# Gated delta rule on Trainium2: key lengths by one-column products, keys turned once, diagonal blocks packed by TensorE before and after one block transpose

## The chip, the cores and the metric

The kernel runs on one core of one Trainium2 chip, in one launch. The metric is the device time of the launch in microseconds. The kernel before took 861.17 us as the median of 3 runs (860.39 to 863.37).

## The reference, cut to what matters

The program is two residual blocks at model width 1024 over 256 tokens, in float32. The first block has two layers: an attention layer and a gated delta-rule layer with 8 heads of width 128. The second block is a wide mixer with a feed-forward network. The change is almost all inside the delta-rule layer.

```python
q = l2_normalize(...); k = l2_normalize(...)          # x * rsqrt(sum(x*x) + 1e-6), per token and head
...
lmat = einsum('bhncd,bhnjd->bhncj', k * beta, k) * decay_strict   # C x C per chunk, C = 64
a_mat = lmat + eye(C)
sol = triangular_solve(a_mat, [v*beta, k*beta*exp(g_cum)], lower=True, unit_diagonal=True)
u, w = sol[..., :Dv], sol[..., Dv:]
a_qk = einsum('bhncd,bhnjd->bhncj', q, k) * decay_incl
for each chunk:  v_new = u - w @ state;  o = (q*exp(g)) @ state + a_qk @ v_new
                 state = state*exp(g_last) + (k*exp(g_last - g)).T @ v_new
```

The kernel works with chunks of 128 tokens, so that there are 16 matrices of 128x128 (8 heads, 2 halves of the sequence). It inverts each triangular matrix by blocks: the 16x16 blocks on the diagonal by VectorE, for all matrices at once, and the larger blocks by products on TensorE.

## The kernel before, in words

The matrices that are multiplied by weights are split in two parts. ScalarE casts each unit of weights (128x1024) to a rounded high part (L1240), VectorE subtracts for the low part (L1838), and TensorE adds three products of 8 matmuls each (L387, and for the last eight units of the stage gdn_in L821, called z_unit 24 to 31). Four slots for the parts go round, and the order of all work is written out by hand on each engine. Each engine runs its instructions in that order, and counting semaphores tie them.

**Before the layer.** After the stage moba_out, GpSimd issues four DMAs of 1 MB each (`late_in`, L2543), with a semaphore for each. TensorE multiplies each of them (`late_products`, L765): number 0 and 1, then `add_partitions` (L617, products of a 128x128 operand with one column of ones), `sum_squares` (L472), and later number 2 and 3.

**The 24 units of q, k and v.** For each unit, ScalarE copies the product to `cin` and to `proj`, and VectorE adds three shifted copies, a short convolution (L2086), before it makes the low part of the unit four further on. After units 17 and 18 ScalarE applies silu to the keys (L1452), after 19 and 20 to the queries.

**The order on TensorE behind unit 23.** Keys turned (natural_k 0, four 128x128 transposes, L838), the decay rows spread over the partitions (L858), natural_k 1, z 24, natural_k 2 and 3, z 25, key-by-key products (gram_k, L868), z 26, values turned (natural_v, L887), z 27, the keys turned a second time (natural_k_again, L848), z 28, z 29, the first key-by-query products (L879), and then the products that turn the inverses (L928). These wait for the diagonal blocks from VectorE (`gdn_scattered`). From there on TensorE builds up the inverses (L939 to L985) between z 30 and z 31, and then the outputs.

**The order on ScalarE there.** A table load, four exponentials (L1492), the key lengths as 16 squares with an accumulator read each (L1478), logarithm and roots of the lengths (L1520 to L1522), the decay exponentials (L1498), z 24 taken out, a table load and silu of the values (L1452), z 25, four copies of 32 partitions for `ct` (L1537), z 26, the values scaled (L1504, these wait for natural_v), z 27, the decayed keys (L1511, these wait for natural_k_again), z 28 and 29.

**The order on VectorE there.** The last convolution and the low part of unit 27, the decay differences (L2126), the triangular matrices `lt` (L2143), the low parts of units 28 and 29, then four block transposes of 32 partitions by 512 elements each, which gather the diagonal blocks (L2153), the small inversions (L2165 to L2202), and four block transposes back into `tt` (L2206).

Of the kernel before, what the change touches and what calls it, by code (L numbers as in the profile page):

```python
# [36 lines left out]
P = 128  # L37
D = 1024
KT = D // P
S = 256  # L40
# [55 lines left out]
for _name, _count in PARAMS:  # L96
# [6 lines left out]
          ("pick", 31), ("parity", 4)]  # L103
# [16 lines left out]
def _program(nc, io, ctx):  # L120
# [34 lines left out]
    def after(name, n):  # L155

        return sem(name), n + start.get(name, 0)
# [53 lines left out]
    cin = [area((S + 3) * u, S + 3) for u in range(GROUP)]  # L211
# [167 lines left out]
    def _(pe):  # L379
# [449 lines left out]

        def natural_k(g):  # L830

            pe.wait_ge(*after("gdn_silu", g // 2 + 1))
            if g < 2:
                pe.wait_ge(taken, all_taken("gdn_in", 23 + g))
            else:
                pe.wait_ge(*after("gdn_length", g - 1))
            for j in range(4):
                mm = pe.transpose(ps[:, 2 + g % 2, j * P:(j + 1) * P], block(8, g, j), ident)  # L838
            mm.then_inc(sem("gdn_natk"), 1)

        def natural_k_again(g):

            if g < 2:
                pe.wait_ge(*after("gdn_length", 3 + g))
            else:
                pe.wait_ge(*after("gdn_vb", 4 * (g + 1)))
            for j in range(4):
                mm = pe.transpose(ps[:, 2 + g, j * P:(j + 1) * P], block(8, g, j), ident)  # L848
            mm.then_inc(sem("gdn_natk"), 1)
# [32 lines left out]
        def natural_v(g):  # L882

            pe.wait_ge(*after("gdn_silu", 4 + g // 2 + 1))
            pe.wait_ge(*after("gdn_lt", g + 1))
            for j in range(4):
                mm = pe.transpose(ps[:, SPREAD[g], j * P:(j + 1) * P], block(16, g, j), ident)  # L887
            mm.then_inc(sem("gdn_natv"), 1)

        natural_k(0)  # L890
        spread_decay()
# [3 lines left out]
        natural_k(2)  # L895
        natural_k(3)
        z_unit(25)
        for g in range(4):
            gram_k(g)
        z_unit(26)  # L900
        for g in range(4):
            natural_v(g)
        z_unit(27)
        for g in range(4):
            natural_k_again(g)
        z_unit(28)
        z_unit(29)
        gram_q(0)
        gram_q(1)

# [13 lines left out]
        pe.wait_ge(*after("gdn_scattered", 4))  # L924
# [8 lines left out]
        pe.wait_ge(*after("gdn_ct", 4))  # L933
# [287 lines left out]
    def _(act):  # L1221
# [232 lines left out]
        for n in range(16, 24):  # L1454
# [7 lines left out]
            if n in (17, 18):  # L1462
                act.wait_ge(*after("conv_free", GROUP + 12 + 4 * (n - 17)))
                silu(8 + 4 * (n - 17))
            if n in (19, 20):
                silu(4 * (n - 19))
# [6 lines left out]

        def lengths(g):

            act.wait_ge(*after("gdn_natk", g + 1))
            for j in range(4):
                ins = act.activation(vb[:, 4 * g + j, :], ps[:, 2 + g % 2, j * P:(j + 1) * P], ACT.Square,  # L1478
                                     accum_out=column(1, 4 * g + j))
            ins.then_inc(sem("gdn_length"), 1)  # L1480
# [26 lines left out]
        def decayed_k(g):  # L1507

            act.wait_ge(*after("gdn_natk", 4 + g + 1))
            for j in range(4):  # L1510
                act.activation(kdg[:, 4 * g + j, :], ps[:, 2 + g, j * P:(j + 1) * P], ACT.Copy,  # L1511
                               scale=column(0, 4 * g + j)).then_inc(sem("gdn_kdg"), 1)
# [4 lines left out]
        for g in range(4):  # L1517
            lengths(g)
        act.wait_ge(*after("gdn_length", 4))
        link(act.activation(kcol[:, 1, :], kcol[:, 1, :], ACT.Ln, bias=eps_col(EPS)))  # L1520
        act.activation(kcol[:, 2, :], kcol[:, 1, :], ACT.Exp, scale=-1.0).then_inc(sem("gdn_root"), 1)
        act.activation(kcol[:, 3, :], kcol[:, 1, :], ACT.Exp, scale=0.5).then_inc(sem("gdn_root"), 1)  # L1522
        for g in range(4):
            decay(g)
# [6 lines left out]
        z_out(25)  # L1531
        act.wait_ge(*after("gdn_zero", 1))
        act.wait_ge(*after("gdn_lt", 4))
        for b in range(4):
            c = slice(32 * (b % 2) + 16, 32 * (b % 2) + 32)
            r = slice(32 * b, 32 * b + 32)
            act.activation(ct[r, :, c], lt[r, :, 32 * b + 16:32 * b + 32], ACT.Copy, scale=parity(2)[r, :]  # L1537
                           ).then_inc(sem("gdn_ct"), 1)
        z_out(26)
        act.wait_ge(*after("gdn_root", 3))  # L1540
        for g in range(4):
            scaled_v(g)
        z_out(27)
        for g in range(4):
            decayed_k(g)
# [22 lines left out]
        act.wait_ge(*after("gdn_scattered", 4))  # L1568
# [251 lines left out]
    def _(dve):  # L1820
# [285 lines left out]
        project("gdn_in", conv, first_group=1, groups=5)  # L2106
# [24 lines left out]
        dve.wait_ge(*after("gdn_col_done", 1))  # L2131
        for g in range(4):
            diff(g)
        dve.tensor_tensor(kcol[:, 0, 0:8], gcol[:, 32:40], gcol[:, 0:8], ALU.subtract).then_inc(sem("gdn_kx"), 1)
        dve.tensor_copy(kcol[:, 0, 8:16], gcol[:, 8:16]).then_inc(sem("gdn_kx"), 1)
# [10 lines left out]
        low("gdn_in", 28)  # L2146
        low("gdn_in", 29)

        dve.wait_ge(*after("gdn_zero", 4))
        dve.wait_ge(*after("gdn_lt", 4))  # L2150
        for b in range(4):
            r = slice(32 * b, 32 * b + 32)
            ins = dve.transpose(gathered[r].rearrange("p c (h m) -> p c h m", h=2),  # L2153
                                lt[r, :, 32 * b:32 * b + 32].rearrange("p m (h c) -> p c h m", h=2))
        link(ins)
# [8 lines left out]

        link(dve.tensor_scalar(square16(corner), gathered[:, :, 0:16], parity(0), None, ALU.mult))  # L2165
# [37 lines left out]
        dve.wait_ge(*after("gdn_zero", 2))  # L2203
        for b in range(4):
            r = slice(32 * b, 32 * b + 32)
            dve.transpose(tt[r, :, 32 * (b % 2):32 * (b % 2) + 32].rearrange("p m (h c) -> p c h m", h=2),  # L2206
                          gathered[r].rearrange("p c (h m) -> p c h m", h=2)).then_inc(sem("gdn_scattered"), 1)
# [317 lines left out]
    def _(pool):  # L2525
# [16 lines left out]
        for p in range(4):  # L2542
            pool.dma_start(late_in[p], io["ada_late"][p]).then_inc(sem(f"late_in{p}"), 16)  # L2543
# [4 lines left out]
        pool.memset(tt, 0.0).then_inc(sem("gdn_zero"), 1)  # L2548
        pool.memset(inverse, 0.0).then_inc(sem("gdn_zero"), 1)
        pool.wait_ge(*after("gdn_zero", 3))  # L2550
# [29 lines left out]
def _constants():  # L2580
# [3 lines left out]
    even = np.where(np.arange(P) % 32 < 16, 1.0, 0.0)  # L2584
    out = {
# [7 lines left out]
        "parity": np.stack([-even, even - 1.0, even, 1.0 - even], 1),  # L2593
# [130 lines left out]
```

## Time and profile before

| | |
|---|---|
| median of 3 runs | 861.17 us |
| lowest, highest | 860.39, 863.37 us |
| the profiled execution | 862.46 us |
| its span of instructions | 860.7 us |
| TensorE busy | 829.7 us, 96% of the span |
| VectorE, ScalarE busy | 615.2 us, 485.3 us |
| mean granted TensorE clock | 0.991 |

The profile shows one execution. All times in it are counted from the start of the span. "Clock" is the share of full speed that was granted to TensorE: 1.00 is 2.4 GHz and 0.50 is 1.2 GHz.

### The profile page before, as it was taken

What the parts mean: (1) busy time and instruction counts of PE and PEld (TensorE: products, weight loads), DVE (VectorE), ACT (ScalarE), POOL (GpSimd) and SP (SyncE); (2) the same over time, 40 slices, a digit from 0 to 9 for tenths busy, and PEclk for the clock granted to TensorE, in tenths of its full rate; (3) what the DMA queues carried; (4) which work ended last, traced back from release to release, by engine and by line L of the source; (5) the groups of instructions that cost most, each with busy time, mean ns of one, the idle gap of its engine ahead of it and who ended that gap; (6) DMA issues with size and microseconds to landing.
All of it is one profiled execution on the core that took longest, in us unless ns stands there. A gap on an engine that the chain in (4) does not pass through costs nothing.

```text
span 860.7 us, 17680 instructions
## 1 busy us (share of the span) xinstructions
PE 829.7 (96%) x6594; PEld 770.8 (90%) x6594; DVE 615.2 (71%) x1054; ACT 485.3 (56%) x898; POOL 63.8 (7%) x70
## 2 busy tenths in 40 slices
PE   6999999999998999999999979999999999999997
PEld 3899988889998998989898859999999999999885
DVE  4487966687899765976867656665678797788543
ACT  3444565476699455584665436656746644555534
POOL 1000001400010002220000022100002020000000
PEclk9999999999999999999999989999999999999999
DMA  9899962804552121533543425444464455455521
GB/s 375 366 369 381 379 241 92 359 23 155 176 185 99 50 100 50 196 133 121 189 161 132 147 86 190 166 145 148 148 221 159 167 174 187 153 188 195 196 98 49
DMA packets 22012, 153.85 MB, mean 179 GB/s; under 512 B 2496, under 2 KB 2752, under 8 KB 3904
## 3 DMA queue, kind: packets, MB, share of 16 engines
q1 hardware_dynamic: 20592, 145.69, 46.4%
q0 software_dynamic: 1360, 7.34, 2.4%
q8 instruction: 41, 0.67, 0.3%
q14 instruction: 19, 0.16, 0.0%
HBM read 151.97 MB, written 1.05 MB: 178 GB/s over the span
## 4 chain that ended last, share of the span: by engine, by line
PE 82%; DVE 7%; ACT 4%; DMA 3%; issue 2%; POOL 0%; DVEq 0%; SPq 0%; ACTq 0%
PE ps L387 40%; PE ps L1200 7%; PE ps L480 6%; PE ps L458 4%; PE ps L421 3%; DVE w_lo L1838 3%; DMA raw<-in_mixed 2%; ACT w_hi L1240 1%; PE ps L430 1%; PE ps L450 1%; PE ps L821 1%; PE ps L631 1%; PE ps L661 1%; PE ps L554 1%; PE ps L577 1%
## 5 line engine op out<-in xcount | busy, mean ns | idle before, releaser
L1838 DVE TENSOR_TENSOR w_lo<-raw,w_hi 128x1024 fp32r<-128x1024 f32 x230 | 284.8, 1244 | 110.8 <-ACT w_hi L1240 110.0
L1240 ACT CAST w_hi<-raw 128x1024 fp32r<-128x1024 f32 (+1 forms) x230 | 239.8, 1050 | 167.9 <-PE ps L387 62.1
L387 PE MATMUL ps<-in_hi,w_hi 128*128 128x256 f32 x1128 | 163.2, 287 | 3.5 <-DVE w_lo L1838 2.2
L387 PE MATMUL ps<-in_lo,w_hi 128*128 128x256 f32 x1128 | 158.3, 283 | 0.0
L387 PE MATMUL ps<-in_hi,w_lo 128*128 128x256 f32 x1128 | 158.3, 283 | 0.0
L387 PEld LDWEIGHTS ps<-in_hi,w_hi 128*128 128x128 f32 x1128 | 146.1, 192 | 9.3 <-DVE w_lo L1838 4.5
L387 PEld LDWEIGHTS ps<-in_hi,w_lo 128*128 128x128 f32 x1128 | 145.5, 192 | 0.0
L387 PEld LDWEIGHTS ps<-in_lo,w_hi 128*128 128x128 f32 x1128 | 145.5, 192 | 0.0
L2086 DVE SCALAR_TENSOR_TENSOR proj<-work,params,proj 128x256 f32 (+1 forms) x72 | 35.5, 493 | 8.0 <-ACT proj L1436 1.8
L1200 PE MATMUL ps<-w_hi,in_lo 128*128 128x512 f32 x88 | 34.2, 389 | 0.0
L1200 PE MATMUL ps<-w_hi,in_hi 128*128 128x512 f32 x88 | 34.2, 389 | 0.0
L1915 DVE SCALAR_TENSOR_TENSOR work<-raw,cs,work 128x1024 f32 x24 | 30.8, 1284 | 4.8 <-DVE w_lo L1838 2.3
L1200 PE MATMUL ps<-w_lo,in_hi 128*128 128x512 f32 x88 | 34.2, 389 | 0.0
L480 PE MATMUL ps<-w_hi,in_hi 128*128 128x512 f32 x80 | 32.5, 407 | 0.0
L480 PE MATMUL ps<-w_hi,in_lo 128*128 128x512 f32 x80 | 31.2, 391 | 0.0
L480 PE MATMUL ps<-w_lo,in_hi 128*128 128x512 f32 x80 | 31.2, 390 | 0.0
L421 PE MATMUL ps<-in_hi,w_hi 128*128 128x256 f32 x108 | 28.0, 297 | 1.4 <-DVE proj L2270 1.0
L421 PE MATMUL ps<-in_hi,w_lo 128*128 128x256 f32 x108 | 27.3, 291 | 0.0
L1734 ACT ACTIVATE proj<-ps,params 128x256 f32<-128x256 f32 x24 | 11.3, 469 | 28.4 <-PE ps L387 28.3
L2474 DVE SCALAR_TENSOR_TENSOR work<-work,params 128x256 f32<-128x256 f32 x44 | 21.3, 484 | 6.4 <-DVE work L2471 1.2
L421 PEld LDWEIGHTS ps<-in_hi,w_hi 128*128 128x128 f32 x108 | 21.7, 201 | 2.2 <-DVE proj L2270 1.4
L421 PEld LDWEIGHTS ps<-in_hi,w_lo 128*128 128x128 f32 x108 | 21.7, 201 | 0.1
(413 smaller groups left out, 1334.9 us busy)
## 6 DMA issues: line engine op xcount, KB each, us to landing
raw<-in_mixed SPq DMA_DIRECT2D x24, 1024.0 KB, 6.6
raw<-in_ffn_up SPq DMA_DIRECT2D x22, 1024.0 KB, 4.7
raw<-in_gdn_in SPq DMA_DIRECT2D x16, 1024.0 KB, 4.8
raw<-in_w_in SPq DMA_DIRECT2D x16, 1024.0 KB, 4.7
raw<-in_merge SPq DMA_DIRECT2D x12, 1024.0 KB, 4.7
raw<-in_ffn_down SPq DMA_DIRECT2D x11, 1024.0 KB, 4.7
raw<-in_branch SPq DMA_DIRECT2D x6, 1024.0 KB, 4.7
raw<-in_moba_out SPq DMA_DIRECT2D x4, 1024.0 KB, 6.3
```

Source lines behind the costliest of these rows:

```text
L387: mm = pe.matmul(half(u, 0), w[:, u, k * P:(k + 1) * P], a[:, base + k, :], start=(n == 0 and k == 0), stop=(n == 2 and k == UNIT - 1))
L421: pe.matmul(half(u, 0), w[:, u, k * P:(k + 1) * P], in_hi[:, base + k, :], start=(k == 0 and n == 0), stop=False)
L430: mm = pe.matmul(half(u, 0), w_hi[:, u, k * P:(k + 1) * P], in_lo[:, base + k, :], start=False, stop=(k == UNIT - 1))
L458: mm = pe.matmul(out, w[:, u, b * P:(b + 1) * P], a[:, k, :], start=start and n == 0 and m == 0, stop=stop and n == 2 and m == last)
L480: mm = pe.matmul(ps[:, bank + t, :], a[:, base + k, t * P:(t + 1) * P], w[:, k // 2, cols], start=(k == 0 and m == 0), stop=(k == KT - 1 a ...
L1200: mm = pe.matmul(ps[:, 4 + 2 * t + c, :], a[:, k, t * P:(t + 1) * P], w[:, u, cols], start=False, stop=(k == FT - 1 and w is w_lo))
L1240: act.copy(w_hi[:, u, :], src).then_inc(hi_done, 1)
L1734: act.activation(proj[:, n, :], half(n % GROUP, 0), ACT.Identity, bias=param("merge_b", n)).then_inc(taken, 1)
L1838: dve.tensor_tensor(w_lo[:, u, :], src, w_hi[:, u, :].bitcast(F32), ALU.subtract).then_inc(lo_done, 1)
L1915: dve.scalar_tensor_tensor(a, unit_at(r, i, 8), cs[:, bass.ds((i % 2) * GROUP + u, 1)], a, ALU.mult, ALU.add).then_inc(lo_done, 1)
L2086: ins = dve.scalar_tensor_tensor(tile, cin[u][:, tap:tap + S].rearrange("p (a b) -> p a b", a=1), params[:, bass.ds(i * GROUP + (PCOL["gdn ...
L2474: dve.scalar_tensor_tensor(conved, cin[m][:, t:t + S], tap(t), conved, ALU.mult, ALU.add).then_inc(sem("ffn_conv"), 1)
```

## The change

It makes these edits:

- **Key lengths.** ScalarE squares the silu'd keys, still with features on the partitions, in two instructions of 128x1024 behind the two silus. TensorE multiplies each of the 16 blocks by one column of ones into 16 columns of bank 1. The 16 squares with accumulator reads go.
- **Keys turned once.** natural_k_again goes. ScalarE makes the decayed keys out of the first turning.
- **Packing.** TensorE copies the four 32x32 diagonal blocks of each matrix into bank 6 (`compact`, 16 products of 32x32 by 128 columns). VectorE transposes all 128 partitions by 512 at once, from that bank. On the way back there is one transpose of 128x512 and two masked writes of 128x512. The memset of `tt` goes. `ct` comes from bank 6 in two ScalarE instructions.
- **Order.** gram_k moves ahead of z 25, natural_v is split around z 27, z 29 goes behind the first two gram_q. The convolution of unit 23 and the low parts of units 27 to 29 go behind the gathering transpose, and `cin` of slot 3 gets a place elsewhere.
- **late_in.** The four DMAs have one semaphore in common, and each `late_products` waits for all four.

```diff
 def late_products(p):
-    pe.wait_ge(sem(f"late_in{p}"), 16)
+    pe.wait_ge(sem("late_in"), 16 * 4)
...
+def lengths():
+    pe.wait_ge(*after("gdn_ksq", 2))
+    pe.wait_ge(taken, all_taken("gdn_in", 22))
+    for m in range(MATS):
+        at = S + (m % 2) * 8 + m // 2
+        mm = pe.matmul(ps[:, 1, at:at + 1], vb[:, m, :], one, start=True, stop=True)
+    mm.then_inc(sem("gdn_length"), 1)
 def natural_k(g):
-        pe.wait_ge(*after("gdn_length", g - 1))
+        pe.wait_ge(*after("gdn_kdg", 4 * (g - 1)))
-def natural_k_again(g):
...
 def natural_v(g):
-    pe.wait_ge(*after("gdn_lt", g + 1))
+    pe.wait_ge(*after("gdn_lt", 4))
+    if g == 0:
+        pe.wait_ge(*after("gdn_gathered", 1))
+        pe.wait_ge(*after("gdn_ct", 2))
+def compact(g):
+    pe.wait_ge(*after("gdn_lt", g + 1))
+    for b in range(4):
+        r = slice(32 * b, 32 * b + 32)
+        mm = pe.matmul(ps[r, 6, g * P:(g + 1) * P], ident[r, r], lt[r, 4 * g:4 * g + 4, 32 * b:32 * b + 32], ...)
+    mm.then_inc(sem("gdn_compact"), 1)
 # TensorE's order, before and after
-natural_k(0) spread_decay() natural_k(1) z_unit(24) natural_k(2) natural_k(3) z_unit(25) gram_k(0..3)
-z_unit(26) natural_v(0..3) z_unit(27) natural_k_again(0..3) z_unit(28) z_unit(29) gram_q(0) gram_q(1)
+spread_decay() lengths() natural_k(0) natural_k(1) z_unit(24) natural_k(2) gram_k(0..2) natural_k(3)
+gram_k(3) z_unit(25) compact(0..3) z_unit(26) natural_v(0) natural_v(1) z_unit(27) natural_v(2)
+natural_v(3) z_unit(28) gram_q(0) gram_q(1) z_unit(29)
...
 # ScalarE
     if n in (17, 18):
         silu(8 + 4 * (n - 17))
+        act.wait_ge(*after("gdn_silu", n - 16))
+        act.activation(flat(vb[:, 8 * (n - 17):8 * (n - 16), :]), flat(proj[:, 4 * n - 60:4 * n - 56, :]), ACT.Square)
...
-for g in range(4):
-    lengths(g)
-act.wait_ge(*after("gdn_length", 4))
+act.wait_ge(*after("gdn_length", 1))
+link(act.activation(kcol[:, 1, :], ps[:, 1, S:S + MATS], ACT.Ln, bias=eps_col(EPS)))
 # then, after: roots, exp of kx, decay(0) decayed_k(0) decay(1) decayed_k(1) decay(2) decay(3) z_out(24)
 # decayed_k(2) decayed_k(3) z_out(25), wait gdn_gathered, ct x2, silu of the values x2, scaled_v(0)
 # z_out(26) scaled_v(1) scaled_v(2) z_out(27) scaled_v(3) z_out(28) z_out(29)
...
 # VectorE
-project("gdn_in", conv, first_group=1, groups=5)
+project("gdn_in", conv, first_group=1, groups=4)
+for u in range(3):
+    conv(5, u)
+    low("gdn_in", 24 + u)
...
-low("gdn_in", 28)
-low("gdn_in", 29)
-for b in range(4):
-    r = slice(32 * b, 32 * b + 32)
-    ins = dve.transpose(gathered[r]..., lt[r, :, 32 * b:32 * b + 32]...)
+dve.wait_ge(*after("gdn_compact", 4))
+dve.transpose(gathered..., ps[:, 6, :].rearrange("p (m h c) -> p c h m", h=2, c=16)).then_inc(sem("gdn_gathered"), 1)
+conv(5, 3)
+for n in range(27, 30):
+    low("gdn_in", n)
...
-for b in range(4):
-    dve.transpose(tt[r, :, 32 * (b % 2):32 * (b % 2) + 32]..., gathered[r]...)
+link(dve.transpose(product..., gathered...))
+for b in range(2):
+    dve.tensor_scalar(tt[:, :, 32 * b:32 * b + 32], product..., parity(4 + b), None, ALU.mult)
...
-    pool.dma_start(late_in[p], io["ada_late"][p]).then_inc(sem(f"late_in{p}"), 16)
+    pool.dma_start(late_in[p], io["ada_late"][p]).then_inc(sem("late_in"), 16)
```

## Rows read from the trace of the kernel before

**Rows 1.** The page: busy time, and the chain that ended last, by engine.
```profile
PE 829.7 (96%) x6594; PEld 770.8 (90%) x6594; DVE 615.2 (71%) x1054; ACT 485.3 (56%) x898; POOL 63.8 (7%) x70
PE 82%; DVE 7%; ACT 4%; DMA 3%; issue 2%; POOL 0%; DVEq 0%; SPq 0%; ACTq 0%
```
**Rows 2.** Timeline of TensorE: start us, us, line, out<-in, count [idle before <-releaser].
```profile
251.78 1.15 PE L858 MATMUL ps<-stat,consts 8*128 8x256 f32 x16
...
253.27 1.20 PE L821 MATMUL ps<-in_hi,w_hi 128*128 128x256 f32 x8
...
256.22 0.61 PE L838 MATMUL ps<-consts,proj 128*128 128x128 f32 x4
...
260.58 3.74 PE L868 MATMUL ps<-proj 128*128 128x128 f32 x32
...
267.02 1.91 PE L887 MATMUL ps<-consts,proj 128*128 128x128 f32 x16
...
275.19 0.66 PE L848 MATMUL ps<-consts,proj 128*128 128x128 f32 x4 [2.51 <-ACT core_a L1504]
...
277.00 2.06 PE L821 MATMUL ps<-in_hi,w_hi 128*128 128x256 f32 x8
...
283.82 1.95 PE L879 MATMUL ps<-proj 128*128 128x128 f32 x16
286.62 2.08 PE L928 MATMUL ps<-consts,core_b 64*64 64x64 f32 x64 [0.84 <-DVE core_b L2206]
...
301.73 1.20 PE L959 MATMUL ps<-work 32*32 32x32 f32 x64
```
**Rows 3.** Timeline of VectorE, the same columns.
```profile
250.98 1.74 DVE L2086 SCALAR_TENSOR_TENSOR proj<-work,params,proj 128x256 f32 x3
252.63 1.22 DVE L1838 TENSOR_TENSOR w_lo<-raw,w_hi 128x1024 fp32r<-128x1024 f32 x1
...
257.87 4.22 DVE L2126 SCALAR_TENSOR_TENSOR work<-ps,gcol,consts 128x128 f32<-128x128 f32 x16
...
269.75 4.30 DVE L2153 STREAM_TRANSPOSE core_b<-work 32x512 f32<-32x512 f32 x4
...
281.72 0.35 DVE L2202 TENSOR_SCALAR core_b<-core_a,consts 128x256 f32<-128x256 f32 x1
282.11 4.36 DVE L2206 STREAM_TRANSPOSE core_b<-core_b 32x512 f32<-32x512 f32 x4
```
**Rows 4.** Timeline of ScalarE, the same columns: the table and silu of the values.
```profile
264.07 1.28 ACT L1452 ACT_TABLE_LOAD   x1
265.37 2.01 ACT L1452 ACTIVATE proj<-proj 128x1024 f32<-128x1024 f32 x2
```
**Rows 5.** The late DMAs by their tensor, and the timeline of TensorE beside them.
```profile
L2543 POOL DMA_DIRECT2D proj<-in_ada_late x3: 527/530/533, 147.6 to 148.7; - x3
...
DMA to landing us min/median/max: 5.4/9.8/16.2
...
163.32 1.07 PE L765 MATMUL ps<-memkv,cs_wide 128*32 128x256 f32 x16
...
165.19 1.95 PE L617 MATMUL ps<-consts,work 128*128 128x1 f32 x16
167.00 3.70 PE L472 MATMUL ps<-proj,consts 128*128 128x256 f32 x16
```
**Rows 6.** Windows (PE busy, PEld, DVE, ACT, POOL, clock, DMA) and TensorE's timeline.
```profile
165.00:172.00 7.00, 7.00 (x54) 6.40 (x47) 2.11 (x7) 3.45 (x10) 0.00 (x0) 1.00 0.63 240
274.00:281.00 7.00, 5.43 (x33) 5.20 (x34) 6.48 (x19) 7.00 (x27) 0.00 (x0) 0.76 0.01 2
329.00:335.00 6.00, 4.99 (x37) 4.59 (x30) 5.74 (x11) 5.02 (x16) 1.52 (x2) 0.72 0.02 4
504.00:516.00 12.00, 8.46 (x47) 6.54 (x46) 8.22 (x17) 4.92 (x14) 5.41 (x6) 0.72 0.16 48
...
504.58 1.99 PE L798 MATMUL ps<-rows,consts 4*128 4x256 f32 x8
...
328.44 1.15 PE L1046 MATMUL ps<-stat,consts 1*128 1x256 f32 x16
```

More of the change, by code:

```diff
@@ L210, in _program @@
     ada_rows = [area(4096 + S * n, S) for n in range(2)]
-    cin = [area((S + 3) * u, S + 3) for u in range(GROUP)]
+    cin = [area((S + 3) * u, S + 3) for u in range(GROUP - 1)] + [area(2560, S + 3, of=core_b)]
     fbuf = [area(2048 + 512 * u, 2, S) for u in range(2)]
@@ L895, in _ @@
         natural_k(2)
+        gram_k(0)
+        gram_k(1)
+        gram_k(2)
         natural_k(3)
+        gram_k(3)
+        pe.wait_ge(*after("gdn_root", 1))
         z_unit(25)
         for g in range(4):
-            gram_k(g)
+            compact(g)
         z_unit(26)
-        for g in range(4):
-            natural_v(g)
+        natural_v(0)
+        natural_v(1)
         z_unit(27)
-        for g in range(4):
-            natural_k_again(g)
+        natural_v(2)
+        natural_v(3)
         z_unit(28)
-        z_unit(29)
         gram_q(0)
         gram_q(1)
+        z_unit(29)
         def quarter(q):
@@ L932, in _ @@
         z_unit(30)
[L933 removed]
+        pe.wait_ge(*after("gdn_ct", 2))
         pe.wait_ge(taken, all_taken("gdn_in", 30))
@@ L1472, in column @@
             return kcol[:, n, (m % 2) * 8 + m // 2:(m % 2) * 8 + m // 2 + 1]
[L1474 to L1480, printed above, removed]
         def z_out(n):
@@ L1516, in _ @@
             decay_q(g)
-        for g in range(4):
-            lengths(g)
-        act.wait_ge(*after("gdn_length", 4))
-        link(act.activation(kcol[:, 1, :], kcol[:, 1, :], ACT.Ln, bias=eps_col(EPS)))
+        act.wait_ge(*after("gdn_length", 1))
+        link(act.activation(kcol[:, 1, :], ps[:, 1, S:S + MATS], ACT.Ln, bias=eps_col(EPS)))
         act.activation(kcol[:, 2, :], kcol[:, 1, :], ACT.Exp, scale=-1.0).then_inc(sem("gdn_root"), 1)
         act.activation(kcol[:, 3, :], kcol[:, 1, :], ACT.Exp, scale=0.5).then_inc(sem("gdn_root"), 1)
-        for g in range(4):
-            decay(g)
         act.wait_ge(*after("gdn_kx", 2))
         act.activation(kcol[:, 0, :], kcol[:, 0, :], ACT.Exp).then_inc(sem("gdn_root"), 1)
-        z_out(24)
+        act.wait_ge(*after("gdn_root", 3))
+        decay(0)
+        decayed_k(0)
+        decay(1)
+        decayed_k(1)
+        decay(2)
+        decay(3)
+        z_out(24)
+        decayed_k(2)
+        decayed_k(3)
+        z_out(25)
+        act.wait_ge(*after("gdn_zero", 1))
+        act.wait_ge(*after("gdn_gathered", 1))
+        for b in range(2):
+            act.activation(ct[:, :, 32 * b + 16:32 * b + 32], ps[:, 6, :].rearrange("p (m c) -> p m c", c=32)[:, :, 16:32],
+                           ACT.Copy, scale=parity(6 + b)).then_inc(sem("gdn_ct"), 1)
         for b in range(2):
@@ L2163, in diagonal @@
                 "p n (i j) -> p n i j", j=16)[:, :, :, 0:w]
+        dve.wait_ge(*after("gdn_gathered", 1))
         link(dve.tensor_scalar(square16(corner), gathered[:, :, 0:16], parity(0), None, ALU.mult))
@@ L2202, in _ @@
         link(dve.tensor_scalar(gathered[:, :, 16:32], square16(inverse), parity(3), None, ALU.mult))
[L2203 to L2207, printed above, removed]
+        link(dve.transpose(product.rearrange("p (m h c) -> p c h m", h=2, c=16),
+                           gathered.rearrange("p c (h m) -> p c h m", h=2)))
+        for b in range(2):
+            dve.tensor_scalar(tt[:, :, 32 * b:32 * b + 32], product.rearrange("p (m c) -> p m c", c=32), parity(4 + b), None,
+                              ALU.mult).then_inc(sem("gdn_scattered"), 1)
         def masked_q(g):
@@ L2584, in _constants @@
     even = np.where(np.arange(P) % 32 < 16, 1.0, 0.0)
+    left = np.where(np.arange(P) % 64 < 32, 1.0, 0.0)
     out = {
```

58 lines of the change are left out of this document (23 added, 35 removed).

## The prediction

> **What bounds the kernel now.** I read the page first: TensorE is busy for 96% of the span and carries 82% of the chain that ended last [rows 1]. So a saving counts only where TensorE waits, or where its own work shrinks. Then I went through the chain between the last q/k/v unit (ended at 250.63 us) and the products of L928 at 286.62, since almost every edit lies there. In that stretch the timeline of TensorE shows three losses: 2.5 us of waiting in the second turning of the keys, for the scaled values of ScalarE, a slow stretch behind it (8 matmuls in 2.06 us at 277.00, where the same eight take 1.20 at 253.27), and 0.84 us in front of L928, where it waits for VectorE's last block transposes [rows 2]. VectorE is busy nearly all the time there: eight block transposes take 4.30 and 4.36 us [rows 3]. Behind 286.62 TensorE runs on almost without a wait to 326 us, so what L928 gains or loses goes to the end. I last looked for waits that the change touches outside this stretch, and found one, at 163 us (below).
>
> The sum is made against the profiled execution: 862.46 us, of which 860.7 is the span and 1.8 lies around it. It stands 1.3 us above the median of the runs, 861.17. I carry the difference over to the median.
>
> **The layer, step by step, with full clock.** Prices: a z unit 2.95 us (253.27 to 256.22), four turnings 0.42, four gram_k 3.5 (32 records begin within 3.5 of the 3.74), so 0.87 each, the spreading 1.1 to 1.25, two gram_q 1.9 [rows 2]. One convolution is 1.65 (250.98 to 252.63), a low part 1.14, four decay differences 4.1, one gathering transpose of 32x512 1.07, the small inversions 8.0 (274.07 to 282.11) [rows 3]. Three operations are not in the trace:
>
> - The key lengths are 16 products of a 128x128 operand with one column, 32 records. The nearest row has the very shape: L617 took 1.81 us for 16 records (165.19 to 167.00) [rows 5]. That gives 3.5 us, and 3.4 to 3.7 as bounds.
> - `compact` is 16 products in 32x32 tiles with 128 columns. A record with 128 columns takes 0.11 us in gram_k [rows 2], so 32 of them with nothing overlapped would be 3.5 us, and with the four tiles side by side 0.9. L959 shows that such tiles do overlap, with 64 records of 32 columns in about 1.1 us, 0.017 each [rows 2]. I take 1.05, near the lower end, since each of the four tiles reads and writes partitions of its own; the bounds are 0.9 and 3.5.
> - One block transpose of 128x512 in place of four of 32x512. The bounds are 1.07, if the four groups of 32 partitions go side by side, and 4.3, if not. I take 1.07: the other operations of VectorE take all 128 partitions at once (128x256 in 0.35 us), and each of the four transposes already has the full 512 elements per partition [rows 3]. The two masked writes of 128x512 are twice that length, 0.55 each.
>
> The Trainium skill ("Vector Engine (DVE) Microarchitecture Reference", section on the reshape front-end) says that each bank of 32 channels has its own 32x32 reorder array, by which the four groups go side by side. No row here has a block transpose over 128 partitions, so only the run can show it; by the page it would be 1.07 again.
>
> With these prices TensorE goes: spreading from 251.2, lengths 252.4 to 255.9, two turnings to 256.8, z 24 to 259.7, a turning and three gram_k to 262.8, a turning and gram_k 3 to 264.1, z 25 to 267.0. VectorE starts the differences 3.3 us sooner (254.6 for 257.9), since a convolution and a low part are put off, and I allow 0.7 us of delay from the two squares on ScalarE (1.0 us each) behind units 17 and 18. It then waits for gram_k and has the fourth `lt` at 265.3. `compact` is only issued behind z 25, so it runs 267.0 to 268.05, and the gathering ends at 269.3, when the old one would have been at 269.75, its start. VectorE then owes a convolution (1.65) and three low parts (3.4): 274.4. The inversions end at 282.4, the transpose and the two writes at 284.65. That is 1.8 us sooner than before, although 6.5 us of transposes are gone, because the work put off lies in between and because of the wait for `compact`.
>
> TensorE meanwhile does z 26 to 271.0 and waits at natural_v(0) for silu of the values, which ScalarE can begin only after `gdn_gathered`, two copies (0.65) and a table load of 1.28; silu itself is 1.0 [rows 4]. That is 272.4, a new wait of 1.45 us. Then two turnings to 273.3, z 27 to 276.25, two turnings to 277.1, z 28 to 280.0, gram_q to 281.9, z 29 to 284.9. L928 starts at 284.9 for 286.62: **1.7 us saved**. Both engines arrive within 0.3 us of one another, so an error in either takes from the gain and cannot add to it. The 2.5 us wait goes because the keys are turned once, and what is late next is silu of the values on ScalarE, then VectorE's inversion.
>
> What else moves costs nothing here: the memset of `tt` is GpSimd's, long done; SP's next load waits for the low parts of units 26 and 27, now some 15 us later, but it fetches gdn_out units not cast before 308 us.
>
> **The late DMAs.** TensorE comes to late_products(0) at 163.32, when its own DMA has long landed. The last of the four was issued at 148.7 and took the longest, 16.2 us: it lands at 164.9 [rows 5]. With one semaphore TensorE stands until then. Behind it come L617 and L472, and L472 ends the chain of the layer norm, so nothing takes up the delay: **1.5 us lost**. If the DMAs land sooner or later in another run it is 0.5 to 2.5.
>
> **The clock.** With full clock the two give −1.7 + 1.5 = −0.2 us. But in the new order TensorE does, from 250.6 to 255.9, nothing but products of 8 rows and of one column. In the trace the granted clock fell to 0.50, that is 1.2 GHz, three times. Once it was behind a wait (274 to 281). Twice it fell with hardly any wait: at 330 behind the one-row products of L1046 and 1.3 us of idling, and near 508 behind four-row products (504.58) followed by 64-row ones, with TensorE busy all along [rows 6]. The mean clock of these windows, 0.76, 0.72 and 0.72, makes 3.4, 3.4 and 6.7 us at the low level. Against a fall speaks that two blocks of 1.8 us of one-column products (165 to 172) ran at 1.00, but they had 5 us of full products with them. Five unbroken microseconds of thin work are more than any of these rows has.
> One such stretch of 3.4 us takes half of itself from TensorE: 1.7 us, on a chain where everything behind waits for it. Two or three in a row, since the one-column products go on at half speed, take 3.4 to 5.1.
> The Trainium skill ("TensorE: Matmul & The Clock Gate", "What's actually happening") says that the gate opens and closes by how busy TensorE has been. By that rule alone the unbroken one-column products hold the clock, and this is the first rival. The trace does not bear it out for thin products: near 508 the clock fell while TensorE was busy.
>
> **The rivals.**
>
> - *The clock falls for one stretch* (forecast): −1.7 + 1.5 + 1.7 = +1.5 us, 862.7. For it: the falls at 330 and 508, two of the three lasting 3.4 us.
> - *The clock holds*: −0.2, 861.0. For it: the one-column blocks at 165 and 171. Against it: they were short and mixed.
> - *The clock falls for two stretches or more* (slower): +3.2 to +4.9, 864.4 to 866.1. Its place is the lengths block itself; it decides if the fall comes while more than half of the 16 products are still to go, since they then take 0.21 us a record in place of 0.11.
> - *The late wait costs nothing and the clock holds*: −1.7 or, if silu comes in time too, −2.0, where VectorE's end at 284.65 stops it: 859.5 to 859.2. Against it: the landing time in rows 5.
> - *One transpose costs as much as four*, so that the packing does not do what it says: 3.2 us more at each end of VectorE's path, of which 0.3 is slack, and 1.5 for the late wait: about +6, 867.
>
> **How the numbers follow.** Chances: forecast 0.35, the clock holds 0.28, two stretches or more 0.24, late wait free 0.09, transposes not parallel 0.04. 0.3% of this kernel is 2.6 us, about what a measurement can tell from no change. The forecast at +1.5 and the clock-holds case at −0.2 both lie inside it, with an error of about 1 us each: of 0.63, 0.53 stays within, 0.06 is slower, 0.04 faster. The two-stretch case is slower for 0.22 of its 0.24. The case without a late wait is faster for 0.03 of its 0.09, since it lacks 0.6 us to the bound. With the last case that makes faster 0.07, same 0.61, slower 0.32. I move it to 0.12, 0.54 and 0.34, for what no case here holds. The range runs from 859.2 (no late wait, the clock holding) to 866.0 (three low stretches); the forecast's own is 861.7 to 863.7.
>
> **What would show each step.** L765 starts at about 165 us behind a wait of 1.5 us for a DMA. The lengths block takes 3.5 us at full clock and more at half; a window from 252 to 262 us (253.5 to 263.5 with the shift) has a mean clock of 0.7 to 0.85 if the clock fell, 1.00 if not. `compact` takes about 1 us, each block transpose 1.07 and not 4.3. Natural_v(0) waits 1 to 1.5 us for silu (L1452). L928 starts 34.3 us after the last unit's end if the clock holds and 36.0 with one low stretch; before it was 36.0 too (250.63 to 286.62). I am wrong if L765 starts without a wait, if the clock holds, or if TensorE finds a longer wait than silu's.

## The result

The changed kernel takes **864.84 us** (median of 7 runs, 863.84 to 866.9) where the kernel before takes 861.32 (7 runs). The ratio is **1.0043**, 95% interval 1.0029 to 1.0056: 0.4% slower, 3.5 us by the medians. The forecast was +1.5 us (862.7); the value lies in the case of two low stretches or more (864.4 to 866.1). The profiled execution took 865.39 us, of which 863.3 is the span. Two executions ran in a slow state, one of the experiment e7 (4589.86 us) and one of the kernel before beside it (1016.45 us), and are left out of every number below.

### The profile page after: what moved, and what is told of

Its sections match the earlier page's. It is cut to its first block, busy times and chain, and to the rows that moved or that the text cites. A ratio compares the mean times of both kernels' runs of the same rounds, so it can differ in the third digit from the quotient of the medians.

```text
span 863.3 us, 17707 instructions
## 1 busy us (share of the span) xinstructions
PE 834.9 (97%) x6642; PEld 777.2 (90%) x6642; DVE 608.1 (70%) x1050; ACT 482.1 (56%) x866; POOL 62.8 (7%) x69
## 3 DMA queue, kind: packets, MB, share of 16 engines
HBM read 151.97 MB, written 1.05 MB: 177 GB/s over the span
## 4 chain that ended last, share of the span: by engine, by line
PE 86%; DMA 5%; DVE 4%; ACT 2%; issue 1%; POOL 0%; SPq 0%; DVEq 0%; ACTq 0%; POOLq 0%
PE ps L387 43%; PE ps L1218 7%; PE ps L480 6%; PE ps L458 4%; PE ps L421 3%; PE ps L821 3%; DMA proj<-in_ada_late 2%; PE ps L430 1%; DVE w_lo L1853 1%; PE ps L450 1%; DMA raw<-in_moba_first 1%; DMA proj<-in_ada_first 1%; PE ps L554 1%; PE ps L577 1%; DMA memkv<-in_ada_first 1%
## 5 line engine op out<-in xcount | busy, mean ns | idle before, releaser
L1218 PE MATMUL ps<-w_hi,in_hi 128*128 128x512 f32 x88 | 34.3, 389 | 0.0
L1218 PE MATMUL ps<-w_hi,in_lo 128*128 128x512 f32 x88 | 34.3, 389 | 0.0
L1218 PE MATMUL ps<-w_lo,in_hi 128*128 128x512 f32 x88 | 34.3, 389 | 0.0
L2101 DVE SCALAR_TENSOR_TENSOR proj<-work,params,proj 128x256 f32 (+1 forms) x54 | 26.0, 482 | 5.8 <-ACT proj L1454 1.9
```

Source lines behind the costliest of these rows:

```text
L1218: mm = pe.matmul(ps[:, 4 + 2 * t + c, :], a[:, k, t * P:(t + 1) * P], w[:, u, cols], start=False, stop=(k == FT - 1 and w is w_lo))
L2101: ins = dve.scalar_tensor_tensor(tile, cin[u][:, tap:tap + S].rearrange("p (a b) -> p a b", a=1), params[:, bass.ds(i * GROUP + (PCOL["gdn ...
```

## The profile after

The page: TensorE is busier, VectorE less, and the late DMAs now stand in the chain [rows 1].

```profile
PE 834.9 (97%) x6642; PEld 777.2 (90%) x6642; DVE 608.1 (70%) x1050; ACT 482.1 (56%) x866; POOL 62.8 (7%) x69
PE 86%; DMA 5%; DVE 4%; ACT 2%; issue 1%; POOL 0%; SPq 0%; DVEq 0%; ACTq 0%; POOLq 0%
```

TensorE's timeline from the end of the last q/k/v unit (start us, us, line, count [idle before <-releaser]) answers [rows 2]. L836 are the key lengths, L867 gram_k, L897 `compact`, L889 the value turnings, L946 the products that were L928:

```profile
249.89 0.41 PE L808 MATMUL ps<-consts,rows 8*128 8x8 f32 x4
...
250.38 1.10 PE L857 MATMUL ps<-stat,consts 8*128 8x256 f32 x13
251.41 6.41 PE L836 MATMUL ps<-small,core_a 128*128 128x1 f32 x32
257.69 1.95 PE L847 MATMUL ps<-consts,proj 128*128 128x128 f32 x8
259.29 2.06 PE L821 MATMUL ps<-in_hi,w_hi 128*128 128x256 f32 x8
...
264.02 2.84 PE L867 MATMUL ps<-proj 128*128 128x128 f32 x24
...
271.00 1.07 PE L897 MATMUL ps<-work,consts 32*32 32x128 f32 x32
...
276.29 1.09 PE L889 MATMUL ps<-consts,proj 128*128 128x128 f32 x8 [1.14 <-ACT proj L1470]
...
288.57 2.08 PE L946 MATMUL ps<-consts,core_b 64*64 64x64 f32 x64
```

The same stretch in windows (busy us and count of PE, PEld, DVE, ACT, POOL, then the granted clock, DMA share, GB/s). TensorE is busy 10.00 of 10.00 us at half clock, 1.2 GHz:

```profile
252.00:262.00 10.00, 10.00 (x50) 10.00 (x50) 5.94 (x21) 6.36 (x20) 2.77 (x4) 0.50 0.24 95
262.00:272.00 10.00, 10.00 (x109) 9.67 (x108) 4.23 (x16) 5.34 (x14) 0.00 (x0) 0.98 0.01 2
```

By the trace's record of the granted clock the low stretch runs from 252.08 to 262.32, 10.2 us. It begins 0.7 us into the lengths, which take 6.41 us. The key turnings and z unit 24 behind them, plain full products, are slow too (2.06 for eight where [rows 2] has 1.20). VectorE waits 6.58 us for gram_k (its timeline, answering to [rows 3]), and each block transpose over 128 partitions is short:

```profile
265.17 4.23 DVE L2161 SCALAR_TENSOR_TENSOR work<-ps,kcol,work 128x128 f32<-128x128 f32 x16 [6.58 <-PE ps L867]
272.21 0.72 DVE L2166 STREAM_TRANSPOSE core_b<-ps 128x512 f32<-128x512 f32 x1 [2.81 <-PE ps L897]
...
285.68 1.13 DVE L2219 STREAM_TRANSPOSE core_b<-core_b 128x512 f32<-128x512 f32 x1
286.85 0.88 DVE L2222 TENSOR_SCALAR core_b<-core_b,consts 128x512 f32<-128x512 f32 x2
```

TensorE at the late products, where [rows 5] shows no wait:

```profile
162.57 1.07 PE L765 MATMUL ps<-memkv,cs_wide 128*32 128x256 f32 x16 [1.25 <-DMA proj<-in_ada_late]
```

**The bill of the two profiled executions** (+2.9 us). From the end of the last unit (start of L808) to L928 or L946: 250.63 to 286.62 is 35.99 us before, 249.89 to 288.57 is 38.68 after, +2.7. The late wait: +1.25. TensorE reached the late products 2.0 us sooner (it would have started at 161.32, where the kernel before started at 163.32), in a part that the change leaves alone: −2.0, a difference between two executions. Outside the span 2.1 us for 1.8: +0.3. What is left, some 0.7, lies behind L946.

**Time and clock apart.** Every run lists its span and the mean granted clock over it. As TensorE is busy for 97%, (1 − clock) × span is about what the clock took, and clock × span what the work would take at full clock. (It counts too much where TensorE waits at the low clock, as it does for some 3.2 us near 508 in the kernel before.) The three columns are means over the runs; the standard error of "at full clock" is 0.2 to 0.4 (0.6 for the one with 6 runs), that of "lost to it" 0.3 to 0.8. "Layer" is the stretch of the bill in the profiled execution:

| kernel | runs | median us | ratio to before (95%) | clock | lost to it | at full clock | layer |
|---|---|---|---|---|---|---|---|
| before | 35 | 861.08 | 1 | 0.9915 | 7.3 | 852.3 | 35.99 |
| after | 7 | 864.84 | 1.0043 (1.0029–1.0056) | 0.9876 | 10.7 | 852.4 | 38.68 |
| e1 late apart | 12 | 863.25 | 1.0016 (1.0002–1.0030) | 0.9888 | 9.7 | 851.0 | 35.48 |
| e2 before, joint | 11 | 862.24 | 1.0017 (1.0000–1.0033) | 0.9913 | 7.5 | 853.5 | 36.01 |
| e3 wide lengths | 11 | 860.93 | 0.9988 (0.9976–1.0000) | 0.9935 | 5.5 | 852.8 | 33.93 |
| e4 wide and apart | 12 | 859.91 | 0.9987 (0.9974–1.0000) | 0.9932 | 5.8 | 851.7 | 33.94 |
| e5 e4, z27 first | 12 | 858.94 | 0.9971 (0.9955–0.9987) | 0.9938 | 5.4 | 851.7 | 33.74 |
| e6 e4, back unpacked | 12 | 860.61 | 1.0000 (0.9984–1.0016) | 0.9938 | 5.4 | 853.5 | 35.56 |
| e7 e1, turnings between | 11 | 862.75 | 1.0010 (0.9995–1.0024) | 0.9903 | 8.4 | 852.2 | 37.04 |
| e8 e1, interleaved | 12 | 861.65 | 1.0007 (0.9991–1.0024) | 0.9906 | 8.1 | 851.5 | 36.62 |
| e9 e4, front unpacked | 12 | 862.06 | 1.0007 (0.9994–1.0021) | 0.9906 | 8.1 | 852.1 | 37.25 |
| e10 before, thin | 6 | 867.91 | 1.0079 (1.0057–1.0101) | 0.9863 | 11.8 | 854.4 | 41.72 |
| e11 before, wide | 12 | 863.40 | 1.0019 (1.0009–1.0030) | 0.9919 | 7.0 | 854.4 | 38.77 |
| e12 e5, waits filled | 12 | 858.06 | 0.9967 (0.9951–0.9984) | 0.9936 | 5.5 | 850.8 | 32.59 |

e1 to e4 shared one chip, e5 to e8 a second, e9 to e11 a third, e12 ran on a fourth. The kernel before ran beside them on each, with medians of 860.91 to 861.26, and each ratio is to those runs; its row is that of the first chip. Differences between two experiments on different chips, such as e5, e6 or e9 against e4 and e12 against e5, carry that spread of 0.35 us as well. The first line of the table is the lesson in small: between before and after the work at full clock is equal (852.3 and 852.4), and the clock takes 3.4 us more.

## The experiments

**e2. The late transfers alone, in the kernel before.**

```diff
-            pe.wait_ge(sem(f"late_in{p}"), 16)
+            pe.wait_ge(sem("late_in"), 16 * 4)
```

> The kernel before with the four late transfers on one semaphore, waited for in full: the one line of the change that has nothing to do with the delta layer, alone. Theory: the products of the four transfers start when the last has landed, some 1.3 to 1.5 us later than the first of them did; the time rises by 1.3 to 1.5 us over the kernel before. Rival: the last of them waited already or the start is hidden, 0 to 0.4 us.

Measured: 862.24 us, +1.2 at full clock, with the clock unchanged. TensorE stands 1.34 us ahead of L765. The theory holds, and 1.2 to 1.3 is the size.

**e1. The late transfers apart again, in the changed kernel.** The reverse edit.

> The changed kernel with one semaphore for each of the four late transfers again (to have three semaphores to spare, the columns, lengths, packing and natural_v steps count on one). Nothing else differs. Theory: the wait of 1.25 us that the late products show goes, and the time falls by 1.2 to 1.5 us, to about 863.5 if the changed kernel is at 864.8 on this chip. Rival: a cycle saved that early is taken back, since a later stage waits on its own transfer or on another engine anyway: change under 0.4 us. The delta layer keeps its 38.7 us from the end of the last unit to the diagonal products, and its long low stretch of the clock of about 10 us.

Measured: 863.25 us, 1.6 less than after, 1.4 less at full clock; the wait is gone. What I expected of the clock was wrong: in this profiled execution it fell at 253.61, when the lengths (3.78 us, from 250.06) were all but done, and the layer took 35.48 us. This execution fell once more, though, from 304.81 to 311.64, in products of 32x32 and 64x64, with TensorE busy all the time; the changed kernel ran the same products at 1.00. Added up, the two profiled executions lose the same to the clock (0.986 both). So where and for how long the clock is low varies between executions of the same products. That is why it is judged here by its mean over the runs.

```profile
302.00:305.00 3.00, 3.00 (x109) 2.96 (x100) 2.91 (x7) 1.33 (x3) 0.32 (x1) 0.97 0.65 221
305.00:312.00 7.00, 7.00 (x55) 6.88 (x54) 3.67 (x4) 2.77 (x6) 0.00 (x0) 0.53 0.56 209
```

**e3. The lengths with 128 columns.** More work for the same result:

```diff
-            for m in range(MATS):
-                at = S + (m % 2) * 8 + m // 2
-                mm = pe.matmul(ps[:, 1, at:at + 1], vb[:, m, :], one, start=True, stop=True)
+            for i in range(MATS):
+                at, m = S + i, 2 * (i % 8) + i // 8
+                mm = pe.matmul(ps[:, 1, at:at + 128], vb[:, m, :], ones[:, 0:128], start=True, stop=True)
```

> The changed kernel with the 16 products for the key lengths 128 columns wide instead of one (the same stationary blocks, the moving operand is the matrix of ones; each product but the last is overwritten by the next in all columns but its first, the columns that are read hold the same lengths). It does more work, not less. Theory that the thin products cost through the clock: the low stretch that now begins inside them and lasts 10.24 us is gone or is down to one of 3.4 us, the lengths take 3.5 to 3.9 us instead of 6.41, the step from the last unit's end to the diagonal products falls from 38.7 to 34 to 36 us, and the time falls by 2.5 to 4.5 us against the changed kernel, to 860.3 to 862.3. Rival, that the lengths are slow by themselves (the 32 weight loads, or waits between them) and the clock falls there whatever is issued: the lengths stay above 6 us and the time rises by up to 2 us. Second rival, that the low stretch only moves to the next quiet place, as in the kernel before: the time falls by 1 to 2 us and a stretch of 3.4 us or more stands between 262 and 290 us.

Measured: 860.93 us, 3.9 less than after. The lengths, and the window around them:

```profile
251.36 3.84 PE L836 MATMUL ps<-consts,core_a 128*128 128x128 f32 x32
...
252.00:262.00 10.00, 10.00 (x90) 10.00 (x89) 7.44 (x28) 8.95 (x26) 2.80 (x4) 1.00 0.26 100
```

TensorE is busy 10.00 us in both windows; with one column the clock is 0.50 and 50 matmuls begin, with 128 columns it is 1.00 and 90 begin. The layer falls to 33.93 us. Both rivals fall: the weight loads don't make it slow, and no low stretch appears elsewhere in the layer. At full clock the kernel is not faster than after (852.8 and 852.4); the whole gain is the clock's, 10.7 to 5.5 us. The edit also changes the order of the 16 products; e10 and e11, which share one order, leave the width as the only difference.

**e4. Both.**

> Both edits together: the lengths 128 columns wide, and the late transfers each waited for alone. Theory, that the two causes stand in different stages and add: the time falls by the sum of the two single edits, 3.8 to 6 us under the changed kernel, to 859 to 861; it then stands 0.3 to 2 us under the kernel before. Rival, that they do not add because a stretch of low clock comes back somewhere else: no lower than the better of the two alone.

Measured: 859.91 us, 4.9 less than after, and 1.0 less than e3. The two causes add. The ratio to the kernel before is 0.9987 with an interval that ends at 1.0000, so alone it is not clearly faster.

**e10 and e11. The thin piece in the kernel before**, and the same with 128 columns (`ones[:, 0:128]`). Nobody reads these products.

```diff
         spread_decay()
+        for i in range(MATS):
+            pe.matmul(ps[:, 1, S + i:S + i + 1], ident, ones[:, 0:1], start=True, stop=True)
         natural_k(1)
```

> The kernel before the change with 16 one-column products more (stationary the identity, moving one column of ones, into a bank where nobody reads) behind the 8-row decay products, and nothing else: the thin piece alone, without the rest of the change. Theory: 3.5 us of work, of which up to 2.9 us are absorbed by the waits for ScalarE and VectorE that follow, so 0.6 to 1.5 us at the same clock; and a fall of the clock as in the changed kernel: mean granted clock from 0.991 to 0.988 to 0.990, 1 to 3 us. Together 2 to 4.5 us slower. Rival: the fall came from something else in the change, and the clock stays at 0.991: 0.6 to 1.5 us slower.

> The kernel before the change with the same 16 products more, 128 columns wide: more work than with one column (3.8 us in place of 3.5 us at 2.4 GHz). Theory: the clock does not fall there, mean granted clock 0.991 or above; 0.8 to 1.8 us slower than the kernel before, and 1 to 3 us faster than with the one-column products. Rival, that the clock does not depend on how wide these products are: within 0.5 us of the one-column kernel, and slower than it rather than faster.

Measured: 867.91 us with one column, 863.40 with 128. The work at full clock is the same, 854.4 both (+1.9 over the 852.5 of the kernel before on that chip); what differs is the clock, 11.8 against 7.0 us lost. So 16 one-column products in a row cost this kernel 4.5 us more than 128 times as many columns, and the fall needs nothing else of the change. Not all of the 4.5 need come from the block itself: in the profiled execution of e10 the clock fell at 253.67 for 6.8 us, and again at 291.22 for 3.4 us, behind a wait for VectorE that had grown from 0.84 to 2.20 us:

```profile
290.35 3.00 PE L930 MATMUL ps<-consts,core_b 64*64 64x64 f32 x64 [2.20 <-DVE core_b L2208]
```

The size was beyond my 2 to 4.5 (+6.6), the wide one a little beyond 1.8 (+2.1 by the medians, +1.6 by the ratio), so the waits took up less of the 3.5 us of work than I thought. Windows of the thin and the wide kernel, in this order:

```profile
252.00:262.00 10.00, 10.00 (x63) 10.00 (x62) 7.89 (x22) 3.68 (x24) 4.13 (x4) 0.66 0.41 160
```
```profile
252.00:262.00 10.00, 10.00 (x88) 10.00 (x88) 8.25 (x24) 6.64 (x42) 4.16 (x4) 1.00 0.44 165
```

**e7 and e8. Breaking the thin piece up.** e7 puts `lengths()` behind `natural_k(1)`; e8 puts one key turning behind every second product:

```diff
...
+                if m % 2:
+                    g, j = m // 8, m // 2 % 4
+                    tr = pe.transpose(ps[:, 2 + g, j * P:(j + 1) * P], block(8, g, j), ident)
...
-        natural_k(0)
-        natural_k(1)
```

> The changed kernel with separate late transfers, one-column lengths, and the eight key transposes (0.98 us, 128 columns each) moved between the 8-row decay products and the lengths instead of behind the lengths. Theory, that the clock falls because 16 products of few rows, 5 small transposes and the 16 one-column products stand in one piece of some 5 us: broken in two, the fall comes less often or for less long; mean granted clock over the runs rises from 0.989 to 0.990 to 0.992 and the time falls by 1 to 2.5 us against the one without the move. Rival: the 3.5 us of one-column products bring it down by themselves: clock 0.989 as before, and the same time to 0.5 us. The logarithm starts 1 us later on ScalarE, which has the slack of the 2.5 us that VectorE waits there.

> The changed kernel with separate late transfers, one-column lengths, and one key transpose of 128 columns behind every second length product. Same products, other order. Theory, that it is the columns that TensorE streams over the piece that hold the clock: the piece of one-column products is thinned by 0.98 us of transposes in 4.5 us; the mean granted clock rises from 0.989 to about 0.990 to 0.992, the time falls by 1 to 2.5 us. Rival: interleaving changes nothing, since the piece still holds too few columns: 0.989, the same time.

Measured: both raise the mean clock as far as expected, to 0.9903 and 0.9906 from 0.9888, and both still fall for 6.8 us in the profiled execution. By the medians e8 (861.65) is 1.6 us under e1 and e7 (862.75) only 0.5, short of the 1 to 2.5 expected, since at full clock it takes 1.2 us more, a price I had set at nothing and have not traced. They ran on another chip than e1, and the intervals of the three ratios overlap, so no gain in time is shown for either. Order helps the clock by 1.3 to 1.6 us; width gave back 5.2.

**e6. The way back undone**, on e4: four transposes of 32 partitions straight into `tt`.

```diff
...
-        link(dve.transpose(product..., gathered...))
-        for b in range(2):
-            dve.tensor_scalar(tt[:, :, 32 * b:32 * b + 32], ..., parity(4 + b), None, ALU.mult)
+        for b in range(4):
+            dve.transpose(tt[r, :, 32 * (b % 2):32 * (b % 2) + 32]..., gathered[r]...)
```

> The kernel with wide lengths and separate late transfers, with the way back undone: four transposes of 32 channels straight into the cleared tt, as before the change, in place of one of 128 channels and two masked writes. Theory: the four take 4.36 us as before the change, where the one and the two writes take 2.05 us; VectorE is 2.3 us later, 0.83 us of it was slack, so TensorE waits 1.4 to 1.5 us ahead of the 64 products of the blocks, and the time rises by about 1.5 us against the same kernel with the way back packed. Rival one: VectorE was further ahead than it looks or the wait is taken back by a later one: 0 to 0.5 us. Rival two: the idle time of TensorE ahead of the thin 64 products also brings down the clock: 3 us or more.

Measured: 860.61 us. That is only 0.7 over the median of e4, with which it was to be compared, but e4 ran on another chip; by the means it is 1.2. Against e5, on the same chip and with e4's work at full clock, it is 1.7. At full clock it is 1.8 over e4, the clock unchanged; the layer takes 1.6 more. VectorE's four transposes, and TensorE's wait:

```profile
279.64 4.38 DVE L2225 STREAM_TRANSPOSE core_b<-core_b 32x512 f32<-32x512 f32 x4
...
284.16 2.08 PE L949 MATMUL ps<-consts,core_b 64*64 64x64 f32 x64 [1.56 <-DVE core_b L2225]
```

The theory holds in size (1.4 to 1.5) and place. The packing on the way back is worth 1.6 us here.

**e9. The way there undone**, on e4: no `compact`, four transposes of 32 partitions from `lt`, four copies into `ct`.

```diff
-        for g in range(4):
-            compact(g)
...
```

> The kernel with wide lengths and separate late transfers, with the way there undone: no packing by TensorE, four transposes of 32 channels straight from the decayed Gram matrices, and four copies of 32 channels into ct, as before the change. Theory: TensorE saves 1.08 us of packing but gains nothing by it. The transposes start 2.8 us earlier on VectorE and take 4.3 us in place of 0.72 us, so VectorE is 0.8 us later, within its slack; ScalarE's copies take 2.09 us in place of 0.84 us and end 0.6 us later, silu after them too, and TensorE's wait for silu after unit 26 grows from 1.15 us to some 2.8 us. Against the same kernel with the way there packed: 0.4 to 0.8 us slower. Rival one: the packing is a cost on TensorE's path, and without it the time falls by 1.0 us. Rival two: the 2.8 us of idle TensorE bring the clock down as the waits before the change did: mean granted clock from 0.993 to 0.991, and 2 us slower or more.

Measured: 862.06 us, 2.2 more than e4. Its work at full clock is up by 0.4, as the theory said; the clock takes 2.3 more, as rival two said. Both are seen in TensorE's wait and the window:

```profile
271.60 1.97 PE L889 MATMUL ps<-consts,proj 128*128 128x128 f32 x8 [2.90 <-ACT proj L1468]
...
269.00:279.00 10.00, 7.40 (x41) 7.41 (x41) 9.50 (x22) 7.07 (x15) 0.00 (x0) 0.66 0.54 211
```

The low stretch, 6.8 us, begins at 270.88, 2.2 us into the wait. So here a wait of 2.9 us brought the clock down as thin products did. The 2.5 us wait of the kernel before [rows 2] also has a low stretch behind it (275.83 to 279.24), but no run takes that wait out alone, and in e10 a wait of 2.20 us ahead of 278.92 passed at 1.00. What `compact` buys is not VectorE's time but the shorter wait for silu.

**e5. Unit 27 ahead of the value turnings**, on e4.

```diff
         z_unit(26)
+        z_unit(27)
         natural_v(0)
         natural_v(1)
-        z_unit(27)
```

> The kernel with wide lengths and separate late transfers, and one step of TensorE moved: unit 27 of the z projection ahead of the first two groups of value transposes, which waited 1.15 us for ScalarE's silu after unit 26. Theory: unit 27 fills that wait; the diagonal products can start 1.15 us earlier on TensorE's side, but VectorE's masked writes end only 0.83 us before TensorE asks for them, so the gain is 0.8 us and the rest shows as a wait of about 0.3 us for VectorE ahead of the 64 products of the blocks. Against the same kernel without the move: 0.6 to 0.9 us faster. Rival: the value products for ScalarE come later, and TensorE waits for its scaled values or for the copy of unit 26 instead: 0 or slower.

Measured: 858.94 us, but at full clock the same 851.7 as e4, and the layer only 0.2 us shorter. The wait of 1.15 us became 0.39 for `w_lo` (VectorE) and 0.27 for ScalarE's copy of unit 26. Forecast missed: half the rival came true. The 1.0 us between the medians is not explained by the layer: the means differ by 0.7, of which 0.4 is clock and 0.3 time outside the span, on two chips.

**e12. Those two waits filled**, on e5.

```diff
+        low("gdn_in", 27)
+        low("gdn_in", 28)
         dve.wait_ge(*after("gdn_zero", 3))
         dve.wait_ge(*after("gdn_compact", 4))
...
+        z_out(26)
         scaled_v(0)
-        z_out(26)
```

> The kernel with unit 27 ahead of the value transposes, and the two waits that stood there taken out: VectorE makes the low halves of units 27 and 28 in the 2.8 us in which it waits for the packing, instead of behind the transpose, and ScalarE copies unit 26 out in the 1.96 us in which it waits for the value transposes. Theory: TensorE's waits of 0.39 us for w_lo and 0.27 us for the copy of unit 26 go, VectorE reaches its masked writes some 2 us earlier and nothing waits for them: 0.5 to 0.7 us faster than the kernel with unit 27 moved alone (858.9), about 858.3, and 2.5 to 3.3 us under the kernel before; mean granted clock 0.993 to 0.994. Rival: the low half of unit 28 is not ready in that gap (its high half comes late from ScalarE), the transpose is held up behind it, and nothing or less than 0.2 us is won.

Measured: 858.06 us; 0.9 under e5 both by median and at full clock, a little beyond the 0.5 to 0.7 expected; the layer 32.59. Units 26 and 27 follow without a gap, and VectorE's wait ahead of the transpose is down from 2.81 to 0.54:

```profile
268.63 1.12 PE L824 MATMUL ps<-in_hi,w_lo 128*128 128x256 f32 x8
269.60 1.12 PE L824 MATMUL ps<-in_hi,w_hi 128*128 128x256 f32 x8
...
266.82 0.72 DVE L2171 STREAM_TRANSPOSE core_b<-ps 128x512 f32<-128x512 f32 x1 [0.54 <-PE ps L900]
```

This version beats both kernels: 0.9967 of the kernel before (0.9951 to 0.9984), some 3 us or 0.3%, and 6.8 us under the changed one by the medians.

## Why the prediction was right or wrong

**Right in sign and mechanism, too small in one term.** The step that failed is the choice of the clock's term: "the clock falls for one stretch", 3.4 us low for +1.7. It was low for 10.2 us there in the profiled execution, and over the runs it took 3.4 us more than before. That is the third case of the prediction, to which I gave 0.24. Its own test, that the fall comes while more than half of the 16 products are still to go, was met: 0.7 us into 3.5. But e10 fell when only a fifth was left, and was low for 6.8 us, so half the block is not where it is decided.

**Part of the closeness is luck.** Two errors went against each other. The work at full clock was forecast 1.5 us up: the layer at 34.3, which is 35.99 less its low stretch of 1.7 and so no change, and 1.5 for the DMAs. By the table it rose by 0.1 (standard error 0.4). The clock's share was forecast as no net change, one low stretch gone and one come, and rose by 3.4.

**One reading that the choice rested on was wrong.** I wrote that near 508 the clock fell "with TensorE busy all along". The window [rows 6] has it busy for 8.46 of 12.00 us, and the timeline of the kernel before shows a wait:

```profile
506.50 1.14 PE L554 MATMUL ps<-proj 64*128 64x256 f32 x8
511.17 2.08 PE L554 MATMUL ps<-proj 64*128 64x256 f32 x8 [3.54 <-DVE work L2416]
```

The low stretch begins at 507.93, 0.3 us into that wait, and a wait of 3.45 to 3.81 us stands there in every other trace of this case too, each with its fall inside it. This row did not speak for a fall under thin work alone; the first that does is the changed kernel's own window.

**What the term is made of.** With the keys turned once, the 2.5 us wait and the slow unit at 277 [rows 2, 6] went, and the low stretch there with them. e3, the change without its thin products, loses 5.5 us where the kernel before loses 7.3. So the rest of the change gave 1.8 us of clock back and the one-column lengths took 5.2 (5.5 to 10.7): net +3.4. Which falls these sums are made of is less sure, since the one near 330 comes and goes as well (below). I had counted the first in the layer's −1.7 and set the second at one third of its size.

**The other terms.**
- *Layer at full clock*: predicted 34.3 us from the last unit's end to L946; e3 measured 33.93. Right. The terms in it: lengths 3.5 for 3.78 (e1); `compact` 1.05 for 1.07; transpose over 128 partitions 1.07 for 1.13, but 0.72 out of PSUM; a masked write 0.55 for 0.44; the wait for silu 1.45 for 1.14. I had TensorE and VectorE arrive within 0.3 us; the slack is 0.83 in e3 (writes end at 282.94, L946 starts at 283.77), with which the wait in e6 agrees. The lengths' term was also added up wrong: twice the 1.81 us of its row is 3.6, not 3.5.
- *Late DMAs*: +1.5 predicted, 1.25 in the profile, 1.2 and 1.4 in e2 and e1. Right.
- *The clock holds*, the rival at 0.28, failed. The Trainium skill ("TensorE: Matmul & The Clock Gate", "What's actually happening") ties the gate to how busy TensorE has been, and by that the thin block would have held it. The windows of this case speak against that reading: busy 10.00 of 10.00 us at 0.50, and 1.00 when only the number of columns grows.
- *One transpose costs as much as four* failed: one of 128 partitions takes 1.13 us, one of 32 takes 1.07 [rows 3]. The Trainium skill ("Vector Engine (DVE) Microarchitecture Reference", "The reshape front-end and per-opcode configuration") has a 32x32 reorder array in front of each bank of 32 channels, and the trace agrees with it: 1.13 us for all four groups.

**Open.** The fall near 330 us that both kernels show [rows 6] is missing in e3, e4, e6, e8, e9, e10, e11 and e12, though nothing was changed there; in e1, e2, e5 and e7 it is present. That may be part of the gain of those that lack it, and I have no cause for it, nor for the fall at 304.81 in e1. The fall near 505 is in all of them, inside that wait of about 3.5 us. Nor is it settled what sets the length of a low stretch once it has begun.

## What to carry to other kernels

Price a block of one-column or few-row products with the granted clock, not only with its instructions: read whether the clock holds in it, and if not, widen the moving operand, since here 128 columns cost 0.06 us more than one and saved 3.9 us (e3) and 4.5 us (e11 for e10). A wait of 2.9 us on the engine that bounds the kernel cost itself and a low stretch here (e9), so look at the clock behind such a wait as well. And when an edit swaps several separate waits for one on the last of them, look up the slowest landing, not the median.

## What the runs showed of the hardware

- Products against one column and against 128 columns take nearly the same time at full clock, 3.78 and 3.84 us for 32 records with a 128x128 weight load each (e1, e3).
- The clock can stay at half for 10.2 us under a TensorE that is busy all the time, and on through full-width products (259.29 to 262.32) that run at full speed elsewhere (after).
- The length of a low stretch differs behind nearly the same thin block: 10.2 us (after), 6.8 (e7, e8, e10), 3.4 (e1).
- A block transpose of 128x512 takes 0.72 us out of PSUM and 1.13 us out of SBUF. Before, the four of 32x512 out of SBUF took 1.07 each [rows 3].
